# One norm stage's order on ScalarE, one filler on TensorE and one signal on VectorE, around the router

## The reference

```
h = rmsnorm(x, norm_w) * (1 + sc) + sh
x = x + g * mixer_or_ffn(h)
```

```
logits = (h @ router_w).astype(float32) + router_b      # 256 x 8
top_val, top_idx = lax.top_k(logits, 2)
top_w = softmax(top_val)
out = sum over 8 experts of gates[:, e] * ((silu(h @ wg[e]) * (h @ wu[e])) @ wd[e])
```

## Time and profile before

| | |
|---|---|
| median of 3 executions | 2215.79 us (2211.09 to 2217.93) |
| span of the profiled execution | 2210.3 us |
| PE busy | 2130.1 us, 96% of the span |
| DVE busy | 1730.5 us, 78% |
| ACT busy | 1345.5 us, 61% |
| POOL busy | 106.9 us, 5% |
| chain that ended last | PE 82%, DVE 10%, ACT 3%, DMA 2%, issue 2% |
| DMA | 621.27 MB, mean 281 GB/s |

### The profile page before, as it was taken

One profiled execution on the slowest core, in us unless ns is written; L12 is line 12 of the kernel. 1 busy time (PEld: TensorE's weight loads), 2 busy tenths in 40 slices (PEclk: granted clock), 3 DMA queues, 4 the chain that ended last, 5 costly groups with the idle time before them and its releaser, 6 DMA issues.

```text
span 2210.3 us, 30651 instructions
## 1 busy us (share of the span) xinstructions
PE 2130.1 (96%) x11803; PEld 1807.9 (82%) x11803; DVE 1730.5 (78%) x1691; ACT 1345.5 (61%) x1445; POOL 106.9 (5%) x138
## 2 busy tenths in 40 slices
PE   7999999999999999999999999999999999999995
PEld 6877897789878695998897788888888888888884
DVE  7567667777764764677889888988988888988996
ACT  4754445565434423443684678777777777777874
POOL 2000000000010010101000000000000000000000
PEclk9999999999999999999999999999999999999998
DMA  8854654557876312777765899999999999999994
GB/s 316 290 191 170 222 191 157 181 200 258 299 247 247 134 67 77 272 253 287 246 224 187 296 380 373 393 365 391 363 390 375 383 366 388 378 378 390 368 388 164
DMA packets 249520, 621.27 MB, mean 281 GB/s; under 512 B 13722, under 2 KB 22293, under 8 KB 249366
## 3 DMA queue, kind: packets, MB, share of 16 engines
q1 hardware_dynamic: 229524, 530.29, 65.8%
q0 software_dynamic: 16864, 81.86, 10.4%
q10 hardware_dynamic: 3042, 7.87, 0.9%
HBM read 611.60 MB, written 12.58 MB: 282 GB/s over the span
## 4 chain that ended last, share of the span: by engine, by line
PE 82%; DVE 10%; ACT 3%; DMA 2%; issue 2%; ACTq 0%; POOL 0%; DVEq 0%; POOLq 0%
PE ps L1588 27%; PE ps L1593 14%; PE ps L723 13%; PE ps L769 9%; PE ps L750 6%; DVE ring_low L2359 2%; DVE ada L2368 2%; DVE arena L2368 2%; PE ps L825 2%; ACT arena L1634 1%; DVE arena L2359 1%; PE ps L1559 1%; PE ps L1377 1%; ACT part_high L1637 1%; DMA arena<-in_w_ada 1%
## 5 line engine op out<-in xcount | busy, mean ns | idle before, releaser
L3374 DVE TENSOR_TENSOR w_low<-ring,w_high 128x2048 fp32r<-128x2048 f32 x288 | 655.5, 2288 | 87.3 <-PE ps L1593 66.6
L2324 ACT CAST w_high<-ring 128x2048 fp32r<-128x2048 f32 x288 | 549.1, 1910 | 175.5 <-PE ps L1593 156.5
L1637 ACT CAST part_high<-ring 128x1024 fp32r<-128x1024 f32 x287 | 296.6, 1048 | 282.0 <-PE ps L769 115.0
L1588 PE MATMUL ps<-w_high,tokens_hl 128*128 128x512 f32 x1792 | 449.3, 393 | 2.0 <-ACT w_high L2324 2.0
L2359 DVE TENSOR_TENSOR ring_low<-ring,part_high 128x1024 fp32r<-128x1024 f32 x287 | 341.3, 1218 | 138.3 <-ACT part_high L1637 136.4
L1588 PEld LDWEIGHTS ps<-w_high,tokens_hl 128*128 128x128 f32 x1792 | 334.4, 188 | 70.5 <-ACT w_high L2324 2.2
L769 PE MATMUL ps<-part_high,arena_split 128*128 128x512 f32 x752 | 237.4, 396 | 6.2 <-issue 4.2
L1593 PE MATMUL ps<-w_low,tokens_hl 128*128 128x512 f32 x896 | 240.2, 390 | 0.1
L1588 PE MATMUL ps<-w_high,hidden_hl 128*128 128x512 f32 x896 | 224.0, 392 | 0.0
L1593 PEld LDWEIGHTS ps<-w_low,tokens_hl 128*128 128x128 f32 x896 | 168.3, 188 | 36.3 <-DVE w_low L3374 0.6
L1588 PEld LDWEIGHTS ps<-w_high,hidden_hl 128*128 128x128 f32 x896 | 166.4, 188 | 33.6
(11 more groups left out here) (303 smaller groups left out, 2427.4 us busy)
## 6 DMA issues: line engine op xcount, KB each, us to landing
ring<-in_moe_w_gate SPq DMA_DIRECT2D x96, 1024.0 KB, 7.7
ring<-in_moe_w_up SPq DMA_DIRECT2D x96, 1024.0 KB, 7.9
ring<-in_moe_w_down SPq DMA_DIRECT2D x96, 1024.0 KB, 7.0
slab<-in_ada_w POOLq DMA_DIRECT2D x64, 768.0 KB, 5.5
ring<-in_w_in SPq DMA_DIRECT2D x19, 2048.0 KB, 7.8
ring<-in_w_ff SPq DMA_DIRECT2D x16, 2048.0 KB, 8.7
hT<-in_moe_w_up SPq DMA_DIRECT2D x16, 1024.0 KB, 7.7
hT<-in_moe_w_gate SPq DMA_DIRECT2D x16, 1024.0 KB, 8.3
```

What stands on the lines that cost most here:

```text
L1588: pe.matmul(ps[:, bank, :], acts[:, x_, k0 + k, :], high[:, k, h * 512:(h + 1) * 512], start=(start and k + x_ == 0), stop=False)
L1637: L(nc.scalar.copy(o, i), s)
L2324: nc.scalar.copy(high, whole).then_inc(sem("high_ready"), 1)
L3374: V.tensor_tensor(low, whole, high.bitcast(F32), ALU.subtract).then_inc(sem("low_ready"), 1)
```

## The change

Four edits, three of them at the router and one that also reaches unit 2:

1. `norm_stage`: in units that are not in `H_OF` (2 and 5), ACT now does all four pieces of squares first and the first token tile's odd tiles after them.
2. At the router, one filler now stands right behind the first turn, in bank 4, and the two in front of the second turn are gone. One moved, one dropped.
3. The copy of the round numbers (L3306) signals `vector2` itself.
4. The memset at L3323, which used to signal it after the result rows, is gone.

```diff
             turn_token(5, 0)
+            stay_awake(4, 1)
             for t in range(TT):
                 for k in range(KT):
                     if (t, k) == (0, 4):
-                        stay_awake(7, 2)
                         turn_token(5, 1)
                     h_ready(5, t, k)
...
                 for t in range(TT):
                     for h in range(2):
-                        if u not in H_OF and (t, h) == (1, 1):
-                            turned_odd(u, 0)
                         act.wait_ge(sem("x_added"), 4 * (u - 1) + 2 * t + h + 1)
                         half_squares(u, t, h)
+                if u not in H_OF:
+                    turned_odd(u, 0)
...
-            copy(rounds[:, 0:2], best)
+            copy(rounds[:, 0:2], best, sem("vector2"))
...
             L.settle()
-            L(V.memset(small[:, 638:639], 0.0), sem("vector2"))
             gathered = A(EG, KT, P)
```

## The result

| | median, us | executions | ratio to the kernel before | 95% interval |
|---|---|---|---|---|
| kernel before | 2215.25 | 20 | | |
| changed kernel | 2218.73 | 20 | 1.0017 | 1.0010 to 1.0023 |

The changed kernel is 3.5 us slower (2 to 5 by the interval), within the 0.3% that I had called no change and within the range, but on the other side of zero: the forecast was 0.4 us faster. With 20 executions of each the interval is 3 us wide, so the 0.3% (6.6 us) was too coarse a limit for what can be told from no change. The profiled execution spans 2217.3 us, 7.0 more than before.

A forecast was written before the change was run, and what follows sets the result against it. PE was taken to bound the kernel, its end following the moment PE becomes gapless. -1.2 at the router, +0.8 at unit 2 and 0 elsewhere gave 2215.79 - 0.4 = 2215.4 us, range 2209.5 to 2220.5.

The forecast's parts named there:

- Edit 1 at the router, -1.2: At the router: squares first let the second tile's reciprocal and second turn come earlier, a gain of 1.2 us.
- Edit 2, nothing: At the router: moving one filler and dropping one changes nothing, covered by waits; at most 1.0 us if uncovered.
- the first rival: Slow clock between the router's fillers or in unit 2 eats the gain: price 1.5, 2216.9 us, chance 0.30.
- Edit 1 at unit 2, +0.8: In unit 2: ACT's odd tiles come later and PE's products wait, a loss of 0.8 us.
- Edits 3 and 4, nothing: Start of the rounds: earlier signal gains 0 (bounds 0 to 2.1 us), since DVE's gapless row decides.
- The rival of the signal that pays: Start of the rounds: PE's start, not DVE's row, sets the gapless point; 2.1 us more, 2213.3 us, chance 0.08.
- The step that failed: Behind unit 2: later steps start on what PE's work released, so the 0.8 us loss reaches the end unchanged.
- The term that I had put at nothing: Everything besides the router and unit 2: 0 us in the sum.
- The rival of the slow stretch: At the router's thinner fillers or unit 2's wait: low clock on the products, price 1.5, 2216.9 us, chance 0.30.
- The range: Whole kernel: 2209.5 to 2220.5 us, about 3.5 us of scatter on either side of 2213.3 to 2216.9.
- the cases: Whole kernel: the forecast and four rivals, 2213.3 to 2216.9 us, all said to lie within 2 us of the median before.

The follow-up runs named there:

- e3_signal: Kernel before with only the round numbers signalled by their copy and the memset gone; 2215.62 us, ratio 1.0003.
- e1: Kernel before with ACT's squares ahead of the first tile's odd tiles in unit 2 alone; 2218.61 us, ratio 1.0013.
- e5: Kernel before with ACT's squares first in unit 2 alone, plus one filler behind unit 2's first turn; 2217.51 us, ratio 1.0011.
- e6: Kernel before with ACT's squares first in unit 2 alone, PE taking the even k of the products behind first; 2217.91 us, ratio 1.0008.
- e7: Kernel before with two fillers behind unit 2's first turn; 2219.54 us, ratio 1.0016.
- e13_after_columns: Changed kernel with L840's one-column records spread between the wide products ahead of them; 2217.31 us, ratio 1.0010.
- e16_router_columns: Changed kernel with unit 2 as before and L840's one-column records spread between wide products; 2213.21 us, ratio 0.9990 to the kernel before.
- e12_both: Changed kernel with unit 2 as before and the narrow records of both L840 and L1205 spread between wider ones; 2215.10 us, ratio 0.9996.
- e15_long_delay: Kernel before with five fillers behind unit 2's first turn; 2218.83 us, ratio 1.0013.

## Why the prediction was wrong, point by point

- *Edit 1 at the router, -1.2*: right by the trace, 1.26 us. In the times of the parts it is smaller than their scatter.
- *Edit 2, nothing*: right. The filler ran in the wait for ACT's tile, of which 0.35 us were left, and the second turn waited 0.15 us for x. The clock at the router's products was full in the profile, so the first rival's place was wrong.
- *Edit 1 at unit 2, +0.8*: right as far as it went, 0.83 us in the trace.
- *Edits 3 and 4, nothing*: right, both in the trace and in e3_signal. The rival of the signal that pays is refuted. The reason given was too simple, though: in the kernel before DVE's row isn't gapless up to the piece for which PEld waits at 1250.26. DVE itself had waited 1.41 us for ACT's `w_high` in front of 1247.92.
- **The step that failed** is the one behind unit 2: "each starts on something that this PE work released, so I carry the 0.8 to the end". I took a delay to arrive at the end as it was. One thing in this kernel is not released by PE's work: the moments at which the clock of PE is set. Moved by 0.8 us against them, the narrow products of L840 met a low clock, which lasts 6.8 us and costs 3.3 us, 2.1 of it in the wide products behind them. The term that I had put at nothing was this one. With it the sum is -0.4 + 3.3 = +2.9 us, where +3.5 (median) and +3.2 (mean) were measured. That the same records met a low clock in seven profiles and a full one in six, with the fall between 2.3 and 3.0 us behind L840's first record, is what the traces have for this; the rule by which the clock is set wasn't tested.
- *The rival of the slow stretch* named the clock, but looked for it where the change thins PE's work (2216.9 us, price 1.5). It gave the right sign and the wrong place, and less than half of the price, 3.3 us. The rule of the Trainium skill ("TensorE: Matmul & The Clock Gate", "Part 1: The HAM clock gate") that stands beside it, that the monitor runs free of the kernel's start, would let one expect the fall at L840 in some executions of each kernel. The traces agree only in part: the low stretch at 292 to 298 us lasted 3.4, 6.8 or 10.2 us, but the fall at L840 stands in all six late profiles and in none of the five early ones with L840 and L1205 in their old order.
- *The range* held, but two of its premises didn't: the cases reach to 2.5 us from the median before (2213.3), not 2, and 0.3% isn't the least that can be told from no change.

What stays open. How the kernel comes to lie so steadily against the clock's changes 860 us from its start was not shown; earlier low stretches, whose lengths differ between profiles, may bring it there, but no run tests that. Nor does any run take L1205's fall from a late kernel, so what it adds in the mean isn't known. How often the fall at L840 happens is known only through the mean clocks: the sum with 3.3 for every execution is above the means of e1, e5, e6 and e7 by about 1 us, which a fall in fewer than all executions would explain. And e13_after_columns (+1.7) and e16_router_columns (-2.0) differ by 3.6 us, with standard errors of 0.6 each, where only edit 1 in unit 2 lies between them, for which the traces have 0.8. Their mean clocks, 0.9887 and 0.9897, stand for about 2.2 us more (an estimate: 0.0010 of 2216 us); where these low stretches lie, one profile of each can't tell.

## What to carry to other kernels

Before moving work that delays TensorE, look for long runs of narrow products behind it, even hundreds of microseconds on: here the clock fell in the middle of 32 records one column wide, and within or right behind 32 sixteen wide, and where they lay against its changes was part of the tuned state. Spread such products between wide ones: for L840 this took the same 8.64 us (from the wide products ahead of it to L1468) and kept the clock up in all five profiles. It doesn't promise a gain in the whole, as e12_both and e13_after_columns show. Compare the granted clock of two kernels by stretches also where the change touches nothing. And a helper that serves two places (`norm_stage` here) has to be priced in both: what freed a waiting turn in one delayed a running product in the other.

## What the runs showed of the hardware

- A busy PE doesn't keep its clock: PE was busy for 3.00 of 3 us in the stretch from 861 to 864, with 26 records, and its clock still fell to 0.50; 32 one-column records behind one another were what it was doing. The same records behind one another kept it at 1.00 in six other profiles, at another moment (e15_long_delay: 865 to 868, 29 records). In groups of six or four between 512-column products they left it at 1.00 in all five profiles.
- Most of the fall's cost falls on the wide products behind: L1475, 512 columns wide, took 15.98 us and not 13.90, and L840 itself 4.47 and not 3.63.
- Within or right behind the products 16 columns wide it fell too: from L1205 to L1221 it took 10.6 us at the full clock, 12.3 with 3.4 us at 0.50 (the changed kernel) and 13.9 with 6.8 us (e1_unit2).
- The fall's cost was steadier than the time of an execution. The 138 executions of the kernel before scatter by 2.1 us (standard deviation), yet L840 to L855 took 21.02 to 21.05 us in all seven profiles with the fall and 17.69 or 17.70 in all six without.
